# Two transformer-like blocks on one core: rotations in slices, copies of query parts in another order, and the sliding attention's scores as whole-array products

## The reference, cut to what matters

```python
SEQ, D_MODEL, DEPTH, DEPTH_2 = 512, 1024, 1, 2
D_FF_2, HEAD_DIM, BLOCK = 2816, 64, 128

def second_block(x, ...):
    for l in range(DEPTH_2):
        h = rmsnorm(x, attn_norm[l])
        z = h @ w_in[l]
        (qA, kA, vA, fA, qB, kB, vB, qI, kI, wI,
         qC, kC, vC, gC, qD, kD, vD, gates) = jnp.split(z, split_at, axis=-1)
        yA = forgetting_attention(heads(qA, 8), heads(kA, 8), heads(vA, 8), fA, forget_bias[l])
        yB = dsa_attention(rope(heads(qB, 8), pos), rope(kB[:, :, None], pos)[:, :, 0], vB,
                           rope(heads(qI, 4), pos), rope(kI[:, :, None], pos)[:, :, 0], wI)
        r = retention(rope(heads(qC, 8), pos), rope(heads(kC, 8), pos) * HEAD_DIM ** -0.5, heads(vC, 8))
        yC = head_groupnorm(r, ret_norm[l]) * jax.nn.silu(gC)
        yD = sliding_window_gqa(rope(heads(qD, 8), pos), rope(heads(kD, 2), pos), heads(vD, 2), attn_sinks[l])
        branch = jnp.einsum('bsnc,ncd->bsnd', jnp.stack([yA, yB, yC, yD], axis=2), w_branch[l])
        x = x + jnp.sum(jax.nn.sigmoid(gates) * branch, axis=2) @ w_out[l]
        u = causal_dwconv(rmsnorm(x, ffn_norm[l]) @ w_up[l], conv_w[l], conv_b[l])
        a, b = jnp.split(u, 2, axis=-1)
        x = x + (jax.nn.silu(a) * b) @ w_down[l]
    return rmsnorm(x, final_norm)

def reference(x, mem, ...):
    return second_block(first_block(x, mem, ...), ...)
```

## Time and profile before

| | |
|---|---|
| median of 3 runs | 3037.11 us (3036.61 to 3038.03) |
| the profiled execution | 3039.78 us, its span 3037.8 us |
| granted TensorE clock, mean | 0.997 of full |
| PE busy | 2988.0 us (98%) |
| PEld busy | 2438.1 us (80%) |
| DVE busy | 1391.3 us (46%) |
| ACT busy | 1289.9 us (42%) |
| POOL busy | 1398.2 us (46%) |
| DMA | 287.61 MB, 95 GB/s |

### The profile page before, as it was taken

How to read it: one execution, slowest core, us unless ns; L and a number is a source line. 1 busy time by engine, 2 the same in 40 slices (tenths; PEclk the granted TensorE clock), 3 DMA queues, 4 the chain that set the end, 5 groups by cost and what they waited for, 6 DMA issues and landing times.

```text
span 3037.8 us, 39928 instructions
## 1 busy us (share of the span) xinstructions
PE 2988.0 (98%) x15302; PEld 2438.1 (80%) x15302; DVE 1391.3 (46%) x2189; ACT 1289.9 (42%) x2219; POOL 1398.2 (46%) x1002
## 2 busy tenths in 40 slices
PE   8999999999999999999999999999999999999998
PEld 7778887788888777878888888878787788878887
DVE  7874351421113878562116433168776520264322
ACT  5443443433333446554234444244564533354432
POOL 5345574444444543234455454554332354544543
PEclk9999999999999999999999999999999999999999
DMA  5234242233333423223333333244231233333332
GB/s 158 83 112 144 87 132 91 77 97 97 99 97 85 142 69 89 53 67 87 97 93 99 94 97 99 83 109 138 68 91 42 64 98 97 97 94 97 97 97 71
DMA packets 214891, 287.61 MB, mean 95 GB/s; under 512 B 42682, under 2 KB 122610, under 8 KB 213042
## 3 DMA queue, kind: packets, MB, share of 16 engines
q1 hardware_dynamic: 212210, 279.88, 31.5%
q0 software_dynamic: 880, 2.99, 0.3%
q10 hardware_dynamic: 1616, 2.23, 0.2%
HBM read 269.80 MB, written 4.72 MB: 90 GB/s over the span
## 4 chain that ended last, share of the span: by engine, by line
PE 89%; DVE 6%; ACT 2%; POOL 1%; issue 1%; DMA 0%; ACTq 0%; SPq 0%; DVEq 0%
PE half L732 80%; PE half L1169 1%; PE half L1155 1%; PE half L1226 1%; POOL wL L2917 1%; PE half L1138 1%; PE half L1133 1%; DVE arena L2082 1%; DVE arena L2681 1%; DVE arena L2715 1%; PE half L987 0%; PE half L1004 0%; DVE rms L2073 0%; PE half L1212 0%; DVE arena L2706 0%
## 5 line engine op out<-in xcount | busy, mean ns | idle before, releaser
L2917 POOL TENSOR_TENSOR wL<-slot,wH 128x512 fp32r<-128x512 f32 (+1 forms) x976 | 1366.5, 1407 | 1610.1 <-ACT wH L1336 1609.0
L1336 ACT ACTIVATE wH<-slot 128x512 fp32r<-128x512 f32 (+1 forms) x976 | 603.4, 625 | 1229.3 <-PE half L732 1223.7
L732 PE MATMUL half<-nH,wH 128*128 128x512 f32 x2336 | 922.6, 395 | 8.1 <-POOL wL L2917 3.1
L732 PE MATMUL half<-nH,wL 128*128 128x512 f32 x2336 | 910.2, 390 | 0.0
L732 PE MATMUL half<-nL,wH 128*128 128x512 f32 x2336 | 909.7, 389 | 0.0
L732 PE MATMUL half<-arena_split,wH 128*128 128x512 f32 (+1 forms) x2432 | 735.8, 385 | 1.7 <-issue 0.8
L732 PEld LDWEIGHTS half<-nH,wH 128*128 128x128 f32 x2336 | 438.5, 188 | 119.7 <-issue 20.2
L732 PEld LDWEIGHTS half<-arena_split,wH 128*128 128x128 f32 x2432 | 451.2, 188 | 94.6 <-issue 3.4
L732 PEld LDWEIGHTS half<-nH,wL 128*128 128x128 f32 x2336 | 438.5, 188 | 92.6
L732 PEld LDWEIGHTS half<-nL,wH 128*128 128x128 f32 x2336 | 438.8, 188 | 89.2 <-issue 1.4
L732 PE MATMUL half<-arena_split,wL 128*128 128x512 f32 (+1 forms) x1216 | 466.4, 384 | 0.0
(11 more groups left out here) (351 smaller groups left out, 2656.5 us busy)
## 6 DMA issues: line engine op xcount, KB each, us to landing
slot<-in_w_in SPq DMA_DIRECT2D x344, 256.0 KB, 2.7
slot<-in_w_up SPq DMA_DIRECT2D x440, 128.0 KB, 2.2
slot<-in_w_down SPq DMA_DIRECT2D x132, 256.0 KB, 2.6
slot<-in_w_branch SPq DMA_DIRECT2D x64, 256.0 KB, 2.6
slot<-in_w_out SPq DMA_DIRECT2D x48, 256.0 KB, 2.8
slot<-in_w_gate SPq DMA_DIRECT2D x88, 128.0 KB, 2.1
arena<-arena SPq DMA_DIRECT2D x40, 256.0 KB, 4.4
slot<-in_w_proj_b SPq DMA_DIRECT2D x16, 256.0 KB, 2.9
```

The source lines that it names most:

```text
L732: mm = pe.matmul(dst, lhsT, rhs, start=(k == 0 and m == 0), stop=(k == last and m == 2))
L1336: act.activation(wH[:, p, 0:cols], slot[:, s, 0:cols], ACT.Copy).then_inc(weights_high, 1)
L2917: pool.tensor_tensor(wL[:, p, 0:cols], slot[:, s, 0:cols], plainly(wH[:, p, 0:cols]), ALU.subtract)\
```

## The change

- **Rotation.** Each is 12 DVE instructions of 128x512 (4 by sin, 4 by cos, 4 adds; `rope_slices`). Behind places -1, 0, 1, 2: three each of qB; 4 to 11: one or two each of qC; 13 to 18 and 20: one or two of kC; 24 to 26 two and 27, 28 three of qD.
- **Stacks.** ACT's copies for dsa stand behind places 11, 14, 18, 22, DVE's rests behind 12, 15, 19, 23. The swa scores get the same form: keys' high parts kDH (over the cos and sin tables, a copy of 128x1024 behind place 28), their rests kDL (in place of the keys, after the retention's weighing), a stack for each pair (ACT behind place 29 for the first, slide places -2, 4 and 6 for the others). SP reloads the tables (512 KB) for layer 1.
- **Retained gating** stands inside slide place 1, ahead of `inverse` and `normed`.
- **Gate copies.** The first bank of bgt1a and bgt2a is copied out ahead of `turned`, the other three behind.
- **bup2.** Of its units that ACT rounds in groups 0 and 1, units 4 and 5 are rounded in group 0 and 6 and 7 at the start of group 1.
- **awq1.** Its last unit is done in two parts, and the copy of the first two banks waits for the first part alone.

The diff, cut to its core:

```diff
 TURN_C = 1
-STACK_AT = (9, 11, 17, 21)
+STACK_A = {11: ("dsa", 0), 14: ("dsa", 1), 18: ("dsa", 2), 22: ("dsa", 3), 28: ("key", "swa"), 29: ("swa", 0)}
+STACK_S = {-2: ("swa", 1), 6: ("swa", 3)}
...
-        kBH, kBL, kII, kDD, selb = R(11056, T), R(11568, T), A(17408, T), qz, A(12080, 1152)
-        stack = [R(18432, 2, T), R(26624, 2, T)]
+        kBH, kBL, kII, kDD, selb = R(11056, T), R(11568, T), A(17408, T), qz[:, :, :], A(12080, 1152)
+        stack = {("dsa", 0): R(18432, 2, T), ("dsa", 1): R(26624, 2, T), ("dsa", 2): R(18432, 2, T), ("dsa", 3): R(26624, 2, T),
+                 ("swa", 0): R(18432, 2, T), ("swa", 1): R(24576, 2, T), ("swa", 2): R(11264, 2, T), ("swa", 3): R(12288, 2, T)}
+        tables = consts[:, 4 * P + T:4 * P + 3 * T]
+        kDH, kDL = consts_split[:, 4 * P + T:4 * P + 3 * T].rearrange("p (a b) -> p a b", b=T), qz_split[:, :, :]
...
+                if l + 1 < LAYERS:
+                    sp.wait_ge(S["heads_scores"], (l + 1) * len(STEPS))
+                    sp.dma_start(tables, I["consts"][:, 4 * P + T:4 * P + 3 * T]).then_inc(S["moved"], 16)
...
-                    unit(ps[1], "awq1", k, stream)
+                    if k < KD - 1:
+                        unit(ps[1], "awq1", k, stream)
+                    else:
+                        unit(ps[1], "awq1", k, stream, part=[0, 1]).then_inc(S["bank_done"], 1)
+                        unit(ps[1], "awq1", k, stream, part=[2, 3]).then_inc(weights_used, 1)
...
-                queries = {"fox": Q, "swa": qD}
+                queries = {"fox": Q}
                 nth = l * len(STEPS)
 
                 def keys_at(br, i, p, k0, n):
                     rows = slice(HD * p, HD * p + HD)
-                    return K[rows, i, k0:k0 + n] if br == "fox" else kDD[rows, i // 2, k0:k0 + n]
+                    return K[rows, i, k0:k0 + n]
 
...
+                    if br != "fox":
+                        pe.wait_ge(S["stack_rest"], stacked((br, i), l))
                         for p in range(2):
-                            for m, keys in enumerate((kBH, kBL)):
-                                mm = pe.matmul(half[:, S_AT[p]:S_AT[p] + n], stack[i % 2][:, p, b * P:b * P + P], keys[:, 0:n],
+                            for m, keys in enumerate((kBH, kBL) if br == "dsa" else (kDH[:, i // 2], kDL[:, i // 2])):
+                                mm = pe.matmul(half[:, S_AT[p]:S_AT[p] + n], stack[br, i][:, p, b * P:b * P + P], keys[:, k0:k0 + n],
                                                start=(m == 0), stop=(m == 1))
                         mm.then_inc(S["heads_scores"], 1)
                         return
...
+            act.wait_ge(S["bank_done"], 1)
+            act.activation(xq[:, 4:6, :], banks(1)[:, 0:2, :], ACT.Copy).then_inc(S["xq_read"], 1)
             done(act, "awq1")
...
+                    for n in (1, 2):
+                        if (f"bgt{n}a", KD - 1) in weave.at(it):
+                            done(act, f"bgt{n}a", l)
+                            if n == 1:
+                                read_out(act, "btC", l)
+                            else:
+                                act.wait_ge(S["yc_split"], l + 1)
+                            evac_by_bank(gate_b[n], jobs.half[f"bgt{n}a"], part=[0])
...
+                        act.activation(kDH, kDD, ACT.Copy).then_inc(S["stack_high"], 1)
+                        return
+                    if (br, i) == ("dsa", 0):
                         act.wait_ge(S["roped"], PRIMED + l * 5 + 2)
-                    if i >= 2:
+                    elif br == "dsa" and i >= 2:
                         act.wait_ge(S["heads_scores"], nth + 4 * PAIRS + 4 * (i - 1))
+                    elif (br, i) == ("swa", 0):
+                        act.wait_ge(S["heads_scores"], nth + 4 * PAIRS + 4 * 3)
+                    elif (br, i) == ("swa", 1):
+                        act.wait_ge(S["ret_scores_read"], l * 12 + 12)
+                    elif (br, i) == ("swa", 2):
+                        act.wait_ge(S["yc_split"], l + 1)
+                    whole = qB if br == "dsa" else qD
                     for p in range(2):
                         rows = slice(HD * p, HD * p + HD)
-                        ins = act.activation(stack[i % 2][rows, p, :], qB[rows, i, :], ACT.Copy)
+                        ins = act.activation(stack[br, i][rows, p, :], whole[rows, i, :], ACT.Copy)
...
-                    if it in STACK_AT:
-                        stack_high(STACK_AT.index(it))
+                    if it in STACK_A:
+                        stack_high(*STACK_A[it])
...
                     if n < 3:
-                        evac_by_bank(gate_b[n], h)
+                        evac_by_bank(gate_b[n], h, part=range(1, 4) if n else range(4))
...
+                    if it == 4:
+                        stack_high("swa", 2)
                     woven(WEAVE_S, it, then, gate_read)
+                    if it in STACK_S:
+                        stack_high(*STACK_S[it])
...
-                    if 0 < g < NG - 1:
+                    if g == 1:
+                        round_units("bup2", l, 0, [6, 7], 512)
+                    elif 0 < g < NG - 1:
                         others(f"bup{g + 1}", l)
                     elif g == NG - 1:
                         round_units("bdn0", l, 0, range(SPLITS, 7), 512)
                     act.wait_ge(S["taps_added"], l * NG + g + 1)
                     act.activation(conv[:, p, 0:2, :], conv[:, p, 0:2, :], ACT.Silu).then_inc(S["silu"], 1)
+                    if g == 0:
+                        round_units("bup2", l, 0, [4], 512)
                     act.wait_ge(S["ff_ready"], l * NG + g + 1)
                     round_ff(conv[:, p, 0:2, :], g)
+                    if g == 0:
+                        round_units("bup2", l, 0, [5], 512)
...
+                def rope_slices(name, buf, n, first, count):
+
+                    if first == 0:
+                        dve.wait_ge(S["partners"], l * 320 + 64 * n + 64)
+                        read_out(dve, name, l)
+                    for at in range(first, first + count):
+                        op, j = divmod(at, NB)
+                        if op == 0:
+                            link(dve.tensor_tensor(part[:, j, :], part[:, j, :], C["sin"], ALU.mult))
+                        elif op == 1:
+                            link(dve.tensor_tensor(buf[:, j, :], buf[:, j, :], C["cos"], ALU.mult))
+                        else:
+                            ins = dve.tensor_tensor(buf[:, j, :], buf[:, j, :], part[:, j, :], ALU.add)
+                            if j == NB - 1:
+                                ins.then_inc(S["roped"], 1)
...
+                if l:
+                    dve.wait_ge(S["moved"], 16 * 3)
...
+                def rest_of(br, i):
+
+                    if br == "key":
+                        stack_rest(stacked((br, i), l), (kDL,), (kDD,), (kDH,))
+                        return
+                    of, whole = stack[br, i], qB if br == "dsa" else qD
+                    stack_rest(stacked((br, i), l), (of[second, 0, :], of[first, 1, :]), (whole[first, i, :], whole[second, i, :]),
+                               (of[first, 0, :], of[second, 1, :]))
...
-                        rope(*amid)
+                        amid()
...
+                turned_by = [("bqB", qB, 1, {-1: 3, 0: 3, 1: 3, 2: 3}),
+                             ("bqC", qC, 2, {4: 1, 5: 1, 6: 2, 7: 2, 8: 1, 9: 1, 10: 2, 11: 2}),
+                             ("bkC", kC, 3, {13: 1, 14: 2, 15: 1, 16: 2, 17: 2, 18: 2, 20: 2}),
+                             ("bqD", qD, 4, {24: 2, 25: 2, 26: 2, 27: 3, 28: 3})]
...
-                    woven(WEAVE_A, it, ("bqC", qC, 2, [0]) if it == 6 else None)
-                    if it in pieces:
-                        rope(*pieces[it])
-                    if it - 1 in STACK_AT:
-                        i = STACK_AT.index(it - 1)
-                        of = stack[i % 2]
-                        stack_rest(1 + i, (of[second, 0, :], of[first, 1, :]), (qB[first, i, :], qB[second, i, :]),
-                                   (of[first, 0, :], of[second, 1, :]))
+                    woven(WEAVE_A, it)
+                    for name, buf, n, taken in turned_by:
+                        if it in taken:
+                            rope_slices(name, buf, n, sum(taken[x] for x in taken if x < it), taken[it])
+                    if it - 1 in STACK_A and it < 28:
+                        rest_of(*STACK_A[it - 1])
                 for i in range(1, PAIRS):
                     weigh_retained(i)
+                rest_of("key", "swa")
+                rest_of("swa", 0)
...
+                    woven(WEAVE_S, it, retained_gated if it == TURN_C else None)
+                    if it - 1 in STACK_S:
+                        rest_of(*STACK_S[it - 1])
+                    elif it == 4:
+                        rest_of("swa", 2)
```

77 lines of the change are left out of this document (37 added, 40 removed).

## The result

| | before | changed | ratio |
|---|---|---|---|
| median | 3036.99 us (3036.61 to 3040.72, 6 runs) | 3051.05 us (3048.8 to 3052.97, 6 runs) | 1.0044 (95%: 1.0032 to 1.0055) |
| span of the profiled execution | 3037.8 us | 3050.0 us | +12.2 us |
| granted TensorE clock, mean | 0.997 | 0.996 | |

What follows compares the result with a forecast made beforehand. The prediction took PE's own work plus some 50 us of waits as the bound. From 3039.8 us profiled, gains of 15.5, costs of 13.8 and 2.7 to the median gave 3035.4 us, range 3023 to 3043.5.

Steps and rivals of the forecast that it cites:

- sliding scores: Sliding attention's scores in the stacked form: 0.80 us saved per quad, -6.4 us in both layers (0 to -6.8).
- gating: Projections behind the retained gating: PE's two waits of 0.8 us go, -1.6 us (0 to -1.6).
- bup2: Rounding units 4 and 5 in group 0 removes PE's stall for POOL's rest: 1.75 us a layer, -3.5.
- step 31: Dsa score step whose maxima PE awaits: shorter slices replace DVE's pieces in front, -1.5 us (0 to -1.6).
- step 15: Score step waiting 1.88 us for maxima: rests leave and slices replace pieces, half the wait goes, -1.6 us (0 to -3.8).
- step 16: First stacked score: PE newly waits for both DVE rests, 2.2 us a layer, +4.4 us (0 to 5.4).
- step 7: Fox score: three adds of 0.57 us before its bias lengthen PE's wait by 1.7 a layer, +3.4 (0 to 6.0).
- places 28 to 30: ACT's key copy waits for qD's rotation, delaying PE's turns: 2.5 us a layer, +5.0 us (0 to 8).
- slide place 4: ACT waits for DVE's split before a stack, delaying roundings PE needs: 0.5 us a layer, +1.0 (0 to 2.8).
- the second, in which DVE and POOL get in each other's way: More slices meet POOL's subtractions before four fox scores a layer: +10.4 us, 3045.8 us in all; chance 0.15.
- The first rival: DVE reaches the three costly places early enough to cover late copies: centre 3028 us, 3022.6 if all covered; chance 0.33.
- The rival that the whole-array form is no cheaper: Sliding quads gain nothing from PE's new score form: 6.4 us more, 3041.8 us; chance 0.07.

Runs made afterwards that it cites:

- run 9: The kernel of run 8 with sliding scores back as fp32 products of 64 rows, without their stacks, key copy and rests: 3028.59 us, ratio 0.9963.
- run 12: The kernel of run 8, unchanged, timed again on another chip beside the kernel before: 3023.37 us, ratio 0.9947.
- run 3: Changed kernel with four 128x512 slices at each place where one 128x2048 rotation piece stood, none inside place 6: 3054.19 us, ratio 1.0055.
- run 5: Changed kernel with whole rotation pieces at old places, but qC's first piece behind place 6, not in its middle: 3046.51 us, ratio 1.0020.
- run 6: Changed kernel with each rotation in six 128x1024 instructions, two at each piece's place, none inside place 6: 3051.63 us, ratio 1.0036.
- run 2: Changed kernel with the four rotations back as three 128x2048 DVE instructions each at their old places: 3038.09 us, ratio 1.0000.
- run 8: Changed kernel with whole rotation pieces, later key and first and third sliding-stack copies, old dsa stack places except the first, behind place 10: 3023.46 us, ratio 0.9944.

## Why the prediction was wrong

The forecast was 3035.4 us; measured were 3051.05. By its own steps, both layers together:

| term | forecast | by the traces |
|---|---|---|
| sliding scores | -6.4 | -6.3 by the traces of runs 9 and 12 (5.2 in time) |
| awq1 | -0.9 | -1.3, its wait is gone |
| gating | -1.6 | -1.7, its waits are gone |
| the whole sliding stretch (scores, gating, slide place 4) | -7.0 | -6.7 (0.4 more than its parts, not traced) |
| bup2 | -3.5 | -2.8 |
| step 31 | -1.5 | +0.2 in all: -1.6 for its own wait, +1.5 for a new one of 1.23 us at step 29 of layer 1, behind two slices that took 2.47 us |
| step 15 | -1.6 | -3.2 |
| step 16 | +4.4 | +5.4 |
| step 7 | +3.4 | +6.4 |
| places 28 to 30 | +5.0 | +5.6 |
| slide place 4 | +1.0 | +1.7 |
| steps 9, 11, 13 | not priced | +8.6 |

**The step that failed** is the cost of "Step 7 of fox" and what it left out. It priced the slices in front of a bias as "3 x 0.57 = 1.7 us", a quarter of a piece each, at one place. The runs showed three things in its place. A slice takes 0.60 to 0.72 from start to start with POOL idle and 0.79 to 0.89 on the mean, not 0.57, and the three adds took 4.08 us because POOL subtracted three times beside them; the term's own bound of 6.0 for that case was just passed (6.4). PE's pause grew to 3 us and was followed by 3.4 us at half the clock, 1.5 us more. And the slices behind places 4 to 10 stand each in front of a bias too; the sum had no term for them, though it had noted that DVE's list there is full. Together these are 3.0 + 8.6 = 11.6 of the 15.6 us missed. Steps 29 and 31, 16, bup2, slide place 4 and places 28 to 30 missed by 0.6 to 1.7 each to the slow side, step 15 by 1.6 to the fast one; and 2 us are not in the traces, since the profiled execution lay 2.8 us above its median before and 0.8 with the change.

**The rival that came true** was in substance the second, in which DVE and POOL get in each other's way: its sum was 3045.8 with a chance of 0.15. Its marks were seen, waits at steps 9, 11 and 13 of 1.1 to 1.4 us with biases of 2.1 to 2.5 us in front (layer 0). Of its four points step 15 did not come true: its wait went, and step 11 had one instead. The first rival, in which the late copies are covered, had the highest chance of the three (0.33) and fell: the waits at step 16 and at place 28 are there. But the meetings with POOL are only one part of the loss, as runs 3, 5 and 6 show. The other two are the slices' own extra time and the piece that lost its free place in the middle of place 6. That last one was in the diff (`woven(WEAVE_A, it)` without its third argument), and the prediction did not read it as a move from idle time into the path: some 6 us by runs 2 and 5, though with slices, of which two stood behind place 6, this can't be taken apart from the rest by subtraction.

**Right** were step 16 (2.7 a layer; the bounds were 1.8 to 2.7), places 28 to 30 (2.8 a layer, for 2.5) with its place and releaser, and the sliding groups (0.80 on the mean, for 0.80). For step 16 some of it was luck: with the half clock behind the same wait, as in half of the cases, it costs 4.3, and the sum had no term for the clock anywhere. The prediction did not say that the waits at steps 15 and 16 can both be avoided; with the rests one place earlier they are (run 8). The rival that the whole-array form is no cheaper fell with run 9. The Trainium skill's rule that a change of tiling drains the engine ("TensorEngine Tiling (Array Packing)", section "Key Properties") fits the gain; that it is the drain was not tried apart.

## What to carry to other kernels

A list that is written by hand has free time at particular points, here between the negation and the inverse, where DVE waits for ACT; work belongs there, and the same work one instruction later can be wholly on the path. Cutting an operation into slices buys freedom of place and pays per slice, and each slice can be held by another engine: price it from rows of that size, and ask of every slice what stands behind it. A copy that waits for a late result should go behind the waits of the critical engine and not in front, and one place earlier or later can be worth several microseconds. A pause of the critical engine may bring half the clock behind it or not, from one execution to the next; before a difference of 1 or 2 us between two traces is put down to an edit, look at the clock column of both.
